# Modulation blocks in groups of four, and the first MLP matrix applied before the reciprocal root

## The reference, cut to what matters

```python
def layer(x, cvec, p, ctx):
    sh1, sc1, g1, sh2, sc2, g2 = modulation(cvec, p['w_mod'], p['b_mod'])   # silu(c) @ w_mod + b_mod, 6 x 1024
    h = rmsnorm(x, p['norm1_g']) * (1.0 + sc1) + sh1
    mix, ctx_tensors = token_mixers(h, p, ctx)
    x = x + g1 * mix
    h = rmsnorm(x, p['norm2_g']) * (1.0 + sc2) + sh2
    x = x + g2 * (jnp.square(jax.nn.relu(h @ p['w_mlp1'])) @ p['w_mlp2'])
    return x, ctx_tensors
```

## Time and profile before

| | us |
|---|---|
| median of 3 runs | 1688.12 |
| lowest and highest | 1687.16, 1695.42 |
| the profiled execution | 1693.53 |
| its span | 1691.6 |
| PE busy | 1535.9 (91%) |
| DVE busy | 875.5 (52%) |
| ACT busy | 657.9 (39%) |
| mean granted clock of TensorE | 0.949 |

### The profile page before, as it was taken

The page is one execution under the profiler, slowest core; times in us unless marked ns, Lnnn a source line. Parts: engine busy times, 40 slices in busy tenths (PEclk is TensorE's granted clock), DMA queues, the critical chain, the costliest instruction groups (busy, mean ns, idle before and its releaser), DMA issues.

```text
span 1691.6 us, 21109 instructions
## 1 busy us (share of the span) xinstructions
PE 1535.9 (91%) x8533; PEld 1371.7 (81%) x8533; DVE 875.5 (52%) x1355; ACT 657.9 (39%) x1082; POOL 135.8 (8%) x126
## 2 busy tenths in 40 slices
PE   5888798898999799999997897988989997999998
PEld 2887576777799588888885896877777996999998
DVE  2695345444455644444526884455444656554552
ACT  3444343333353433332424444434433534343341
POOL 0011100333000000000000202013330000000000
PEclk9899898898999899999998998998889998999999
DMA  9435555132334554555555341311324332434331
GB/s 324 130 94 166 156 177 158 50 94 58 111 119 133 187 162 152 170 156 168 156 155 175 102 111 56 87 52 43 94 70 117 112 116 78 129 126 125 125 126 49
DMA packets 186086, 210.20 MB, mean 124 GB/s; under 512 B 10702, under 2 KB 154374, under 8 KB 185990
## 3 DMA queue, kind: packets, MB, share of 16 engines
q1 hardware_dynamic: 185990, 208.86, 39.9%
HBM read 204.90 MB, written 3.93 MB: 123 GB/s over the span
## 4 chain that ended last, share of the span: by engine, by line
PE 77%; DVE 13%; ACT 3%; POOL 2%; issue 2%; DMA 2%; SPq 0%; DVEq 0%; ACTq 0%; POOLq 0%
PE bank L630 20%; PE bank L631 19%; PE bank L632 19%; PE y_ps L872 3%; DVE tb L1480 3%; DVE wlo L1391 2%; PE bank L644 2%; PE bank L645 2%; PE bank L646 2%; PE seg_ps L662 2%; PE y_ps L685 1%; PE y_ps L894 1%; PE bank L662 1%; DVE tb L1420 1%; DMA raw<-in_w_in_dram 1%
## 5 line engine op out<-in xcount | busy, mean ns | idle before, releaser
L1391 DVE TENSOR_TENSOR wlo<-raw,whi 128x1024 fp32r<-128x1024 f32 (+1 forms) x288 | 357.3, 1247 | 355.6 <-ACT whi L1033 354.8
L630 PE MATMUL bank<-ahi,whi 128*128 128x384 f32 x1280 | 446.1, 349 | 35.6 <-DVE alo L1423 20.4
L1033 ACT CAST whi<-raw 128x1024 fp32r<-128x1024 f32 (+1 forms) x288 | 296.5, 1036 | 424.0 <-PE bank L632 314.2
L631 PE MATMUL bank<-alo,whi 128*128 128x384 f32 x1280 | 436.6, 341 | 0.0
L632 PE MATMUL bank<-ahi,wlo 128*128 128x384 f32 x1280 | 436.0, 341 | 0.0
L630 PEld LDWEIGHTS bank<-ahi,whi 128*128 128x128 f32 x1280 | 247.5, 193 | 53.9 <-DVE alo L1423 22.7
L630 PE MATMUL bank<-bhi,whi 128*128 128x384 f32 x768 | 264.7, 345 | 5.0 <-DVE blo L1580 3.3
L631 PE MATMUL bank<-blo,whi 128*128 128x384 f32 x768 | 258.2, 336 | 0.0
L632 PE MATMUL bank<-bhi,wlo 128*128 128x384 f32 x768 | 258.0, 336 | 0.0
L631 PEld LDWEIGHTS bank<-alo,whi 128*128 128x128 f32 x1280 | 247.5, 193 | 1.1 <-issue 1.0
L632 PEld LDWEIGHTS bank<-ahi,wlo 128*128 128x128 f32 x1280 | 246.6, 193 | 0.0
(11 more groups left out here) (212 smaller groups left out, 1453.7 us busy)
## 6 DMA issues: line engine op xcount, KB each, us to landing
raw<-in_w_mlp_dram SPq DMA_DIRECT2D x128, 512.0 KB, 3.6
raw<-in_w_in_dram SPq DMA_DIRECT2D x104, 512.0 KB, 3.8
raw<-in_w_mod_dram SPq DMA_DIRECT2D x96, 512.0 KB, 4.0
raw<-in_w_ssd_o_dram SPq DMA_DIRECT2D x16, 512.0 KB, 3.4
raw<-in_w_out_dram SPq DMA_DIRECT2D x16, 512.0 KB, 3.4
raw<-in_w_pool_o_dram SPq DMA_DIRECT2D x8, 512.0 KB, 3.5
raw<-in_w_attn_o_dram SPq DMA_DIRECT2D x8, 512.0 KB, 3.4
raw<-in_w_in_dram SPq DMA_DIRECT2D x8, 256.0 KB, 4.4
```

Source lines behind the costliest of these rows:

```text
L630: nc.tensor.matmul(dst, uh[:, k, tm_cols(m)], hi[k0 + k], start=first and k == 0, stop=False)
L631: nc.tensor.matmul(dst, uh[:, k, tm_cols(m)], lo[k0 + k], start=False, stop=False)
L1033: nc.scalar.copy(dst, src).then_inc(hi_ready, 1)
L1391: nc.vector.tensor_tensor(rest, full, top.bitcast(F32), ALU.subtract).then_inc(lo_ready, 1)
```

## The change

Modulation blocks go in groups of four (`MOD_GAP`, `FIRST_MOD2`, `NEXT_MOD`). In layer 0 four `mod2` blocks follow each of `xbc` 3, 7, 11 and `pool` 3, and the rest go in pairs in the first eight attention rounds; from `xbc` on until the state-space part, one bank is kept for their sum. For layer 1, four blocks run before layer 0's MLP, forty in ten groups inside it (after blocks 5, 11, ... 59), four before `kvd`. In layer 1 the columns of `mod2` are made behind `q`.

The first MLP matrix is applied to x times `coef`, without the reciprocal root: `ahi` is a scaled copy by ACT (`scaled_hi`), `alo` the difference by DVE (`scaled_lo`), both made row block by row block as `wo` is added to x. The rows of `ahi` and `alo` get two columns more, which hold the shift for the two kinds of token, so each matmul of the first matrix has 386 columns. DVE takes the two columns of the sum out of PSUM as a bias (`hbias`) and multiplies the other 384 by the reciprocal root (`rstd2`); ACT does the ReLU with the bias in two pieces, then the square; DVE's square and difference follow. The last two statistics products come after `mlp` 0.

```diff
-MOD_LATE = 10
-MOD_AT = {16 * q + j: 7 * q + j // 2 for q in range(4) for j in range(1, 15, 2)}
+MOD_GAP = 4
+FIRST_MOD2 = {("xbc", 3): range(0, 4), ("xbc", 7): range(4, 8), ("xbc", 11): range(8, 12), ("pool", 3): range(12, 16),
+              **{("round", i): range(16 + 2 * i, 18 + 2 * i) for i in range(8)}}
+NEXT_MOD = {6 * n + 5: range(MOD_GAP + 4 * n, MOD_GAP + 4 * n + 4) for n in range(10)}
...
     for l, name, i in ORDER:
+        if (l, name, i) == (0, "xbc", 0):
+            free = (0, 1, 2)
+        if (l, name, i) == (0, "gaa", 0):
+            free = (0, 1, 2, 3)
...
-            t = sb(name, [P, KT, T], F32R)
-            return [t[:, k, :] for k in range(KT)]
+            t = sb(name, [P, KT, T + 2], F32R)
+            return t, [t[:, k, 0:T] for k in range(KT)]
...
# PE
-                if l:
-                    mod_columns(l, 1)
                 for kq in range(4):
                     gemm_tm("q", kq, 512)
+                if l:
+                    mod_columns(l, 1)
...
-                stats(l, 1, (6, 7))
...
-                            gemm_cm("mlp", 16 * q + j, ahi, alo, 4 * kh, kh == 0, kh == 1)
+                            gemm_cm("mlp", 16 * q + j, hx, lx, 4 * kh, kh == 0, kh == 1, T + 2)
+                            if j == 0 and q == 0:
+                                stats(l, 1, (6, 7))
...
-                        if l + 1 < DEPTH and (q, j) == (1, 1):
+                        if l + 1 < DEPTH and (q, j) == (1, 9):
                             mod_columns(l + 1, 0)
...
# ACT
+                def scaled_hi(k):
+                    for v, (a, b) in enumerate(SEG):
+                        ins = nc.scalar.activation(ahi[k][:, a:b], xT[:, k, a:b], ACT.Copy, scale=coefs[:, l, 1, k, v:v + 1])
+                    ins.then_inc(h_hi, 1)
...
+                act.wait_ge(modc_ready, l * 2 + 2)
+                nc.scalar.copy(ahi_all[:, :, T:T + 2], modcs[:, l, 24:32, :]).then_inc(shift_hi, 1)
                 for b in range(4):
                     ahead("wo", 2 * b + 1)
                     for m in range(2):
                         squares(l, 1, 2 * b + m)
-                root(1)
-                for j in range(4):
-                    h_rows(1, (2 * j, 2 * j + 1))
-                    weights_to(SPLIT_AT[UNIT[l, "mlp", j]] + 1)
+                        scaled_hi(2 * b + m)
+                ahead("mlp", 0)
+                root(1, rstd2)
...
-                            nc.scalar.activation(tb[:, k % 2, 0:T], bank[BANKS[l, "mlp", 16 * q + k][0]][:, 0:T], ACT.Relu)\
-                                .then_inc(relu_ready, 1)
+                            row = tb[:, 2 + k % 2, 0:T]
+                            for v, (c, d) in enumerate(SEG):
+                                ins = nc.scalar.activation(row[:, c:d], tb[:, k % 2, c:d], ACT.Relu, bias=hbias[:, k % 2, v:v + 1])
+                            ins.then_inc(relu_ready, 1)
...
# DVE
+                def scaled_lo(k):
+                    dve.wait_ge(h_hi, (l * 2 + 1) * KT + k + 1)
+                    for v, (a, b) in enumerate(SEG):
+                        ins = nc.vector.scalar_tensor_tensor(alo[k][:, a:b], xT[:, k, a:b], coef[:, 1, k, v:v + 1],
+                                                             ahi[k][:, a:b].bitcast(F32), ALU.mult, ALU.subtract)
+                    ins.then_inc(h_ready, 1)
...
+                            nc.vector.tensor_copy(hbias[:, m, :], psum[:, T:T + 2])
+                            nc.vector.tensor_tensor(tb[:, m, 0:T], psum[:, 0:T], rstd2, ALU.mult).then_inc(scaled_ready, 1)
...
```

More of the change, by code:

```diff
@@ L72, in unit_order @@
     for l in range(DEPTH):
-        out += run(0, "mod1", 16) if l == 0 else run(l, "mod2", MOD_LATE, 32 - MOD_LATE)
-        out += run(l, "kvd", 4) + run(l, "q", 4) + run(l, "xbc", 12) + run(l, "pool", 4)
-        if l == 0:
-            out += run(0, "mod2", 8)
+        out += run(0, "mod1", 16) if l == 0 else run(l, "mod2", MOD_GAP, 32 - MOD_GAP)
+        out += run(l, "kvd", 4) + run(l, "q", 4)
+        for u in run(l, "xbc", 12) + run(l, "pool", 4):
+            out += [u] + [(0, "mod2", n) for n in FIRST_MOD2.get(u[1:], ()) if l == 0]
         fill = [u for name, n in POOL_FILL for u in run(l, name, n)]
@@ L79, in unit_order @@
             out.append(fill[i])
-            if l == 0:
-                out += run(0, "mod2", 2, 8 + 2 * i)
+            out += [(0, "mod2", n) for n in FIRST_MOD2.get(("round", i), ()) if l == 0]
         for name, n in SSD_FILL:
@@ L509, in _ @@
                         tall(l, "pool", 2 * b + kh, w_in_r, l * D + kh * 512, C_POOL + b * 256)
-                if l == 0:
-                    for i in range(8):
-                        mod(0, "mod2", i)
+                        first_mod2("pool", 2 * b + kh)
                 def gate_unit(name, i):
@@ L580, in _ @@
                         tall(l, "mlp", j, w_m2_r, l * DFF + q * 1024 + kh * 512, b * 256)
-                    if later and j in MOD_AT:
-                        mod(l + 1, *later[MOD_AT[j]])
+                    for n in NEXT_MOD.get(j, ()) if later else ():
+                        mod(l + 1, *later[n])
             sp.wait_ge(state_out, DEPTH * 64)
@@ L627, in gemm_cm @@
                         tile = (l, name, 2 * i + m if first and last else i - i % 2 + m)
-                        dst = (claim(tile) if first else bank[BANKS[tile][0]])[:, 0:T]
+                        dst = (claim(tile) if first else bank[BANKS[tile][0]])[:, 0:cols]
                         for k in range(4):
@@ L729, in _ @@
                         gemm_cm("pool", 2 * b + kh, ahi, alo, 4 * kh, kh == 0, kh == 1)
-                if l == 0:
-                    for i in range(8):
-                        gemm_mod(0, "mod2", i)
+                        first_mod2("pool", 2 * b + kh)
                 pe.wait_ge(qkrot_ready, l + 1)
@@ L1462, in _ @@
                 link(nc.vector.tensor_scalar(nsink, sink, -1.0, None, ALU.mult))
+                ahead("kvd", 3)
+                ahead("q", 3)
                 if l:
                     modulation(l, 1)
-                ahead("kvd", 3)
-                ahead("q", 3)
                 def conv(b):
```

137 lines of the change are left out of this document (77 added, 60 removed).

## The result

The changed kernel takes 1648.2 us (median of 4 runs, 1647.15 to 1648.43) where the kernel before takes 1688.5 (4 runs, 1687.16 to 1695.42) on the same chip: a ratio of 0.9752, 95% interval 0.9725 to 0.9779. The forecast was 1635 with a range of 1621 to 1655. By spans of the profiled executions it is 1691.6 against 1646.5, 45.1 us less, where the sum of the prediction had 53.8. So 8.7 of the 13 us by which the forecast was missed lie in the gain. Most of the rest lies in the base: the sum took off 5.4 us because the profiled execution of before (1693.53) stood that far above a median of three runs, but the changed kernel's profiled execution (1648.43) stands at its median.

What follows compares the result with a forecast made beforehand. TensorE's own instructions and standstills were taken to bound the kernel. Gains less costs summed to 53.8 us off the profiled 1693.5; less 5.4 for the median gave 1634.3, stated as 1635, range 1621 to 1655.

Steps and rivals of the forecast that it cites:

- main case: Whole kernel: the predicted gains arrive, 1622 to 1642 us with 1635 as the predicted time; chance 0.55.
- R1: Rival: the MLP's evacuation becomes late, quarters lose up to 2 us each, about 1648 us; chance 0.14.
- R2: Rival: layer 0's xBC groups and shorter splitting window outweigh the first round's gain, layer 1's start gives half: 1645; chance 0.21.
- part F: Costs in both MLPs: 386 columns add 0.8 ns per matmul, 1.3 us; row stride costs nothing; evacuation stays hidden.
- R3: Rival: 386-column matmuls over rows 1544 bytes apart leave the 384 price; 1717 us at the 512 price; chance 0.05.
- Part A: Ahead of layer 1's MLP: the standstill for the norm goes, 25.6 us become 11.4, gain 14.2 us.
- Part B: Ahead of layer 0's MLP: fewer modulation blocks and no waits, 31.0 us become 13.4, gain 17.6 us.
- Part C: Inside layer 0's MLP: ten groups of four blocks replace 28 singles, 33.9 us become 20.8, gain 13.1 us.
- Part D: Start of layer 1: kvd starts 4.2 us earlier, q another 2.8, 1.0 returns; gain 6.0 us, bounds 0 and 8.
- Part E: Layer 0's xBC and attention: first round nets 1.6 us, last four rounds 2.6; gain 4.2 us, bounds -3 and +8.
- R4: Rival: the wait for the root just moves to the MLP's first tile, returning some 5 us; chance 0.05.

Runs made afterwards that it cites:

- the last experiment: Kernel with MLP operands in arena_s, layer 0's modulation pairs moved to attention rounds 0 to 3 and 8 to 11: 1636.2 us, ratio 0.9665 (0.9687 without the move).
- f1: Kernel before with an unused tensor of 128 bytes per partition allocated ahead of bhi: 1699.2 us against 1692.9, ratio 1.0039.

## Why the prediction was right, step by step

The forecast's mechanism held: no wait on DVE ahead of either MLP, groups as x16 of 1.92 us, the `kvd` wait ended by `alo`, no bracket in the MLPs. One of its signs did not: the matmuls of layer 1's MLP were to stay at 0.1733 to 0.1745 us and came at 0.1757 and 0.1767. The time came out 13 us above the forecast, outside the 1622 to 1642 of the main case. That it lies in the range is luck in part: the range was drawn that wide for R1 and R2, and it was something else that used up the room. Of the 13 us, 5 are the base, as said above; in the later sessions the kernel before had medians of 1692.5 to 1693.8, so the profiled execution had been typical and the median of three runs low. The other 8.7 are missing gain, and one step more than accounts for them. With the durations of the stretches above, the slower pitch costs: 1536 matmuls of 386 columns x 3.3 ns = 5.1 us; 2304 on `bhi` and `blo` x 2.3 ns = 5.3; the other 2304 of 384 columns on `ahi` and `alo` x 1.5 ns = 3.5 (from the wide-rows kernel); 432 of 512 columns x 4.4 ns = 1.9; 144 of 288 columns, about 1 ns each, 0.2. Together 16.0 us, an estimate, where part F had 1.3. (By the same prices the wide rows alone would cost 13, and they cost 11, so it is rather too high.)

**Part F** is the step that failed, a cost put at nothing: "The row stride of 1544 bytes is in no row of before; I take no cost." That was a zero without a bound, and worse, I saw only the stride and not that two columns more move every tensor behind them. R3 came nearest (the matmuls over rows 1544 bytes apart leave the price of 384), but I gave it only the sizes at which it would turn the sign or reach the price of 512, 36 and 54 ns; it came with 3.3, too little for its own mark of 0.18 us. R3 also named the 386-column matmuls alone, and two thirds of the cost fell on others. The evacuation in part F was sized well. The groups by line and shape of the changed kernel, as the earlier trace rows:

```profile
L1368 ACT ACTIVATE tb<-tb,small 128x256 f32<-128x256 f32 x64 | 31.6, 494 | 0.0
L1368 ACT ACTIVATE tb<-tb,small 128x128 f32<-128x128 f32 x64 | 25.7, 402 | 95.0 <-DVE tb L1797 95.0
...
L1797 DVE TENSOR_TENSOR tb<-bank,arena_s 128x384 f32<-128x384 f32 x64 | 35.0, 547 | 0.0
L1796 DVE COPY small<-bank 128x2 f32<-128x2 f32 x64 | 10.0, 156 | 54.1 <-PE bank L638 54.1
```

0.547 and 0.156 us for DVE's product and copy, against 0.55 and 0.17 as estimated; the two ReLU pieces 0.90 us together (0.80 to 0.81 as a pair in the timeline), under the 0.97 that I took. The Trainium skill (ScalarE: Activation LUTs, What ACT_TABLE_LOAD costs) had given about 0.8: here the page was the nearer one. R1 did not happen.

**Part A**, 14.2: 14.5, from 25.6 and 11.1 us to the third block. The whole stretch gained 10.2, since the slow pitch costs 4.3 us in it (768 x 3.3 + 768 x 2.3 ns). **Part B**, 17.6: 17.9, from 31.0 and 13.1. **Part C**, 13.1: 13.1 in the kernel with the new places alone; in the changed one the whole stretch gained 26.9, with 4.3 added back 31.2. All three right; the experiment with the root alone shows that B cannot be had without taking blocks away from the MLP's head. The group's price of 1.92 us and not a single's 1.05, which the prediction took from the row, held in every trace with groups. The Trainium skill (TensorEngine Tiling (Array Packing), Tiling Modes) has four tiles of 32 columns that work in parallel; the traces show two blocks in a row at 1.06 us, the time of one, but four at 1.92. (At the time of one, ten groups would have taken 8.7 us less, not the 10 of the prediction.)

**Part D**, 6.0: 8.1, and with the pitch added back (3.6, by the same prices) 11.7; the kernel with the new places alone has 10.7 here. The `kvd` start came 5.4 us earlier and not 4.2. ACT's first scaling moved up 4.1 us as forecast. The rest is that before, DVE still made a low half of the `kvd` weights behind `alo`, and PE started at 900.64, right after it; now no such split stands there. DVE's timeline of before:

```profile
899.78 0.75 DVE L1391 TENSOR_TENSOR wlo<-raw,whi 128x576 fp32r<-128x576 f32 x1
```

`q` came the 2.8 us nearer that were forecast. With the new places alone, 3.3 us of the gain lie where the prediction did not look, in layer 1's state-space part. The view from its first matmul on `bc_cm` to `wo`'s first statistics, before and with the new places alone:

```profile
1128.73:1378.31 249.58, 234.08 (x1228) 208.46 (x1229) 124.96 (x151) 98.41 (x126) 46.13 (x38) 0.92 0.29 89
1100.20:1346.51 246.31, 228.51 (x1228) 206.06 (x1229) 125.48 (x151) 98.41 (x126) 46.33 (x38) 0.95 0.30 90
```

The granted clock was 0.92 in the first and 0.95 in the second. The changed kernel had 0.95 too (248.24 us), but so had the kernel before with two gaps (247.60 us), and the changed kernel with rows of 1600 bytes had 0.92 (251.50 us). Whether the new places bring the better clock or chance does is not shown.

**Part E**, 4.2: -0.3 as measured, 3.3 with the pitch's 3.6 added back, 3.7 with the new places alone, 2.2 between two traces by undoing it alone. Two of its terms were off: the pool projection ended 6.7 us later and not 4.2, and the late rounds gave next to nothing and not 2.6, because the wait was 1.56 and not 1.01. The state-space part began 1.5 us earlier (291.4 against 292.9), hardly more than the first round. R2's mark appeared (2.80 and 3.34 us on `wlo` in xBC, more than the 4 us named), yet the part stayed above zero. R4 did not happen.

So 14.5 + 31.2 + 11.7 + 3.3 = 60.7, less 15.8 (4.3 in each MLP, 3.6 in the rest of each layer), is 44.9, the sum of the four stretches; the spans have 45.1. With the operands where they lay, the same change takes 1635.6 by its ratio. That this is so near the 1635 of the forecast is in part chance: D's surplus, the price of the 386 columns and the low base cancel. By profiled executions it gained 57.9 us where the sum had 53.8.

## What to carry to other kernels

A change in a tensor's size is a change in the place of everything allocated behind it: compare the start-to-start distance of matmuls that a change does not touch before looking for waits, and give an address effect a bound of its own. When a few elements more per row are needed, put that operand behind the others or in an idle arena, so that every tensor whose matmuls did not change keeps its remainder of 256 bytes. And don't take a base from three runs: their median was 5 us under what later sessions showed. Filling a wait pays only where the chain that ends the wait does not pass on: see what is late next, as in the last experiment.

## What the runs showed of the hardware

- 128 unused bytes ahead of one tensor, no instruction changed, made the kernel 0.39% slower; rows of `ahi` and `alo` 8 bytes longer, which also moved `alo` by 64 and `bhi` by 128 bytes, 0.69%. Per matmul of 384 columns the stretches show 0.1733 against 0.1748 to 0.1767 us, and for 512 columns 0.2269 against up to 0.2333, at a granted clock of 1.00.
- It is a relation between tensors, most likely the two operands: all of the program's SBUF tensors moved by 128 bytes cost nothing (8.32 us for 48). As a moving operand 64 bytes off was free (8.32) and 32 (8.48) and 128 (8.45) were not; as a stationary one, 64 off was the dearest case run (11.20 for 48, against 10.89). Which rule is behind it is open. The Trainium skill (SBUF — State Buffer, SBUF: two separate sides) says that TensorE's port never waits for another engine; nothing here speaks against it, since the effect went with the places of tensors that the matmuls read themselves.
- 386 columns cost 3.1 ns more than 384 also at the good remainder, nearly four times what the slope between 384 and 512 gives.
- The spread of the runs of one kernel (up to 11 us) goes with the mean granted clock (0.942 to 0.954 in the nine runs of f1); in three profiled runs it was a stretch of layer 0's state-space part (330 to 380 us) at 0.75, 0.79 and 0.80, where the others had 0.87 to 0.95.
- Two modulation blocks in a row (128*32 tiles, 512 columns) take 1.06 us, as long as one (1.05); four take 1.92.
